# Order of the split weight products within a chunk: all products with the high parts first, those with the low parts last

## The chip, the cores and the metric

One core of a Trainium2 chip (trn2) runs the whole kernel; the other cores are idle. The metric is the device time of one execution in microseconds, lower is better. Engines are named as in the profile: PE is TensorE (PEld its weight loads), DVE VectorE, ACT ScalarE, POOL GpSimd, SP SyncE, which issues the weight loads from HBM.

## What is computed

One inference step of a two-layer decoder trunk on 256 prompt tokens and 8 single decode tokens, 264 columns in all, with a model width of 2048. Layer 0 is a gated DeltaNet mixer (32 value heads of 128) and a SwiGLU feed-forward layer; after it one shared K/V is projected; layer 1 is sliding-window attention (32 heads of 64, 4 K/V heads) and another feed-forward layer. Everything is float32.

```python
def trunk(x, prompt, ...):
    for i in range(N_A_LAYERS):
        h = rms_norm(x, norm_mix[i])
        y, conv_buf, S = deltanet_mixer(h, ..., w_in_a[i], ..., w_out_a[i])
        x = x + y
        x = x + swiglu_ffn(rms_norm(x, norm_ffn[i]), w_gate_up[i], w_down[i])
    kv = rms_norm(x, norm_kv) @ w_kv
    for j in range(N_B_LAYERS):
        q = (rms_norm(x, norm_mix[i]) @ w_q_b[j])
        o = swa_prompt(q, ...) if prompt else swa_sample(q, ...)
        x = x + o @ w_o_b[j]
        x = x + swiglu_ffn(rms_norm(x, norm_ffn[i]), w_gate_up[i], w_down[i])
    y = rms_norm(x, norm_final)
```

The nine weight matrices (`w_in`, `w_out`, `w_gate_up` and `w_down` of two layers, `w_kv`, `w_q`, `w_o`) make up most of the work, and they are all multiplied in the same way, by the function that is changed.

## The kernel before

**Chunks.** All weights are streamed in chunks of 128 x 1024 values, eight blocks of 128 x 128, 858 chunks in all. Each float32 value is split in two parts of a shorter format (fp32r), which TensorE multiplies in one pass: `split_hi` (L465, on ACT) writes `w_hi`, a rounded copy of `w_raw`, and raises `hi_ready`; `split_lo` (L472, on DVE) writes `w_lo` = `w_raw` - `w_hi` and raises `lo_ready`. The activations are split in the same way into `h_hi` and `h_lo` (in other stages `o_`, `a_`, `ao_`). A block of the product is then three products of 128 x 128 by 128 x 264, accumulated in one PSUM bank: w_hi by x_hi (L484), w_hi by x_lo (L485), w_lo by x_hi (L486). So a chunk is 24 products, each with its own weight load.

**Buffers.** `w_raw` has four buffers, `w_hi` and `w_lo` two each (`SPL`). Both splits of chunk c + 2 wait for `w_used` of chunk c, which the last product of a chunk raises (L490). SP's load of a chunk waits for `lo_ready` four chunks back (`load`, L497). Readers of finished banks also wait for `w_used`, or for later semaphores.

**`tiles`** (L475) issues the products of a chunk. `tl` lists its eight blocks: number of the block in the chunk, bank, the two activation parts, whether the block is the first or last one for its bank. Where other work of TensorE is woven in, a chunk is issued in two calls: with `part` 0, four blocks, and with `part` 1, the other four. With `part` None the whole chunk is issued at once (feed-forward layers, K/V, most of the out and o projections). `ends` is used for the very last chunk of the program alone, whose banks are read one by one.

**What stands between the halves.** In the DeltaNet stage (`turn`, L2094) PE works on the 12 chunks of a group of two heads, and weaves in the small products of the group before: `step(G, 2*j)` (L1911) ahead of the first half of chunk j and `step(G, 2*j + 1)` ahead of the second. The steps are one chain of small products with DVE and ACT in between: an inverse of a triangular matrix (steps 4 to 14), the recurrence over two blocks of tokens and the decode tokens (15 to 21), the outer products for the decode states and the sums of squares (21 to 23). Steps 0, 2, 3, 9 and 20 have no products. There are 16 groups. DVE and ACT have programs of their own with the same step numbers: in the turn of chunk j, ACT issues `split_hi` of chunk j + 1 and then its parts of steps 2j and 2j + 1 (in steps 4 and 16 the other way round), DVE its part of step 2j, then `split_lo` of chunk j + 1, the convolution of the next group's q, k and v (L2241), then step 2j + 1. On all engines the instructions run in the order in which they are written. The q projection and the first eight chunks of the o projection (L1112 to L1141) weave in the attention in the same way, with `attention(i, h)`; the first chunks of the program (`first_turn`, L2121) are cut in two because their activations come in two parts (`norm_lo`).

Names that the next sections use: L1709 is ACT's copy in step 12; L2310 DVE's transposes in the inverse; L1713 ACT's copy in step 14; L2379 DVE's `dec_sel` in step 18, and L2062 the products of step 19 that read it; L2405 the new state `S` of DVE in step 19, and L1909 the outer products of steps 21 to 23, the third of which, in step 21, waits for it; L1662 ACT's logarithm of the next group's sums of squares (step 22), for which L2081 waits in step 23; L1919 step 1, which waits for the normalised q and k (L2262); L993 and L773 the turning of the cached keys and the copy of it.

Of the kernel before, what the change touches and what calls it, by code (L numbers as in the profile page):

```python
# [13 lines left out]
P = 128  # L14
# [42 lines left out]
def yoco_step(nc, x_prompt, x_sample, state_delta, state_conv, cache_k, cache_v, norm_mix, norm_ffn,  # L57
# [6 lines left out]
    T = NP + NB  # L64
# [30 lines left out]
    SPL = 2  # L95
# [22 lines left out]
    with ctx:  # L118
# [8 lines left out]
        bank = lower + [upper[:, i, :] for i in range(4)]  # L127
# [18 lines left out]
        w_hi = sb("w_hi", [P, SPL, ELEMS], F32R)  # L146
        w_lo = sb("w_lo", [P, SPL, ELEMS], F32R)
# [95 lines left out]
        low = ExitStack()  # L243
        with low:
# [6 lines left out]
            part = sb("part", [P, 4, T], F32, low)  # L251
# [42 lines left out]
        hi_ready = sem("hi_ready")  # L294
        lo_ready = sem("lo_ready")
        w_used = sem("w_used")
# [177 lines left out]

        def tiles(pe, c, tl, part=None, ends=None):  # L475


            q, s = c
            if part in (None, 0):
                pe.wait_ge(lo_ready, 4 * q + (s + 1))  # L480
            for n, (t, bk, xh, xl, first, last) in enumerate(tl):
                wh = w_hi[:, s % SPL, t * P:(t + 1) * P]
                wl = w_lo[:, s % SPL, t * P:(t + 1) * P]
                nc.tensor.matmul(bank[bk][:, 0:T], wh, xh, start=first, stop=False)  # L484
                nc.tensor.matmul(bank[bk][:, 0:T], wh, xl, start=False, stop=False)  # L485
                m = nc.tensor.matmul(bank[bk][:, 0:T], wl, xh, start=False, stop=last)  # L486
                if ends is not None and last and n < len(tl) - 1:
                    m.then_inc(ends, 1)
            if part in (None, 1):
                m.then_inc(w_used, 1)  # L490
            return m

        def load(sp, c, *halves):

# [415 lines left out]
        def pe_after_delta(pe):  # L910
# [201 lines left out]
            for i in range(8):  # L1112
                for j in range(4):
                    c = chunk(C_Q, RAW, 0, 4 * i + j)
                    if j == 0:
                        pe.wait_ge(u_read, U_Q + i - 1)
                    if i == 0:
                        pe.wait_ge(unit_lo, split_count("mix1", j))
                    tl = [(2 * kk + n, (2 * (i % 2) if i else 6) + n, h_hi[:, 4 * j + kk, :], h_lo[:, 4 * j + kk, :],
                           j + kk == 0, 4 * j + kk == KT - 1) for kk in range(4) for n in range(2)]  # L1120
                    attention(i, 2 * j)
                    tiles(pe, c, tl[0:4], 0)
                    attention(i, 2 * j + 1)
                    tiles(pe, c, tl[4:8], 1)
            for j in range(8):
                c = chunk(C_O, RAW, 0, j)
                order = [(0, 0), (0, 1), (1, 0), (1, 1), (0, 2), (0, 3), (1, 2), (1, 3)] if j == 0 else [
# [5 lines left out]
                pe.wait_ge(p_lo, 2 * j + (2 if j == 0 else 1))  # L1133
                if j == 0:
                    pe.wait_ge(u_read, U_O - 1)
                tiles(pe, c, tl[0:4], 0)
                attention(8 + j // 4, 2 * (j % 4) + 1)
                if j == 0:
                    pe.wait_ge(u_read, U_O)
                pe.wait_ge(p_lo, 2 * j + 2)  # L1140
                tiles(pe, c, tl[4:8], 1)  # L1141
            columns(C_O, UNIT["o"], U_O, ao_hi, ao_lo, done=8)
            ffn(1)

# [672 lines left out]
        def _(pe):  # L1817
# [18 lines left out]
            for u in range(4):  # L1836
# [5 lines left out]
                             stop=True).then_inc(at_pe, 1)  # L1842
# [251 lines left out]
            def turn(g, G):  # L2094
                for j in range(12):
# [10 lines left out]
                    else:  # L2106
# [3 lines left out]
                        tl = [(2 * kk + n if u else 4 * n + kk, pair + n, h_hi[:, k + kk, :], h_lo[:, k + kk, :],  # L2110
                               k + kk == 0, k + kk == KT - 1) for kk in range(4) for n in range(2)]
                        c = chunk(C_IN, 12, g, j)
                    tiles(pe, c, tl[0:4], 0)
                    if G is not None:
                        step(G, 2 * j + 1)
                    if g is None and j == 0:
                        pe.wait_ge(unit_copied, 3 * GROUPS)
                    tiles(pe, c, tl[4:8], 1)

            def first_turn():  # L2120

                for j in range(12):
# [9 lines left out]
                           k + kk == 0, k + kk == KT - 1) for kk in range(4) for n in range(2)]  # L2132
                    if j < 4:
                        pe.wait_ge(norm_lo, 2 * j + 1)
                    tiles(pe, c, tl[0:4], 0)
                    if j < 4:
                        pe.wait_ge(norm_lo, 2 * j + 2)
                    tiles(pe, c, tl[4:8], 1)
                    if j in (1, 3):
                        b = j // 2  # L2140
                        tiles(pe, first_ba(b), [(t, 6, h_hi[:, 8 * b + t, :], h_lo[:, 8 * b + t, :], b + t == 0,
# [617 lines left out]
```

## Time and profile before

| | |
|---|---|
| time, median of 3 runs (lowest to highest) | 2893.99 us (2893.37 to 2894.33) |
| the profiled execution's own time | 2895.47 us |
| its span, first to last instruction | 2893.6 us |
| PE busy, products | 2870.3 us (99%), 25543 |
| DVE busy | 1795.9 us (62%) |
| ACT busy | 1418.8 us (49%) |
| mean busy share of the DMA engines on the weight queue | 56.9% |
| mean granted clock of TensorE, share of full speed | 0.998 |

How to read it: one execution is recorded, with the start and length of each instruction. A line such as L484 is a line of the program; since all weight products come from `tiles`, the three lines L484 to L486 hold 20,592 of them, and their operands' names tell the stage. The products are pipelined: each is drawn some 0.28 us long while the next one starts earlier, so a busy PE is not one that loses nothing, and the distance between starts has to be read. "upper" stands for PSUM banks of the upper half.

### The profile page before, as it was taken

The numbers are of one execution on the slowest core, as the hardware profiler recorded it, in microseconds if no ns is written. First come the engines' busy times: TensorE is split into PE (matmuls) and PEld (weight loads), VectorE is DVE, ScalarE is ACT, GpSimd is POOL, SyncE is SP. The second block draws the span as 40 slices with busy tenths as digits, with TensorE's granted clock in tenths as the row PEclk, the third lists the DMA queues.
The fourth block names the chain that finished last, engine by engine and source line by source line (L and its number), as shares of the span: only waits on it lengthen the run. The fifth ranks groups of instructions, "written<-read, shape, count | busy, mean of one in ns | idle before, by whom it ended". The sixth has DMA issues, their size and how long they took to land.

```text
span 2893.6 us, 68883 instructions
## 1 busy us (share of the span) xinstructions
PE 2870.3 (99%) x25543; PEld 2794.9 (97%) x25543; DVE 1795.9 (62%) x2868; ACT 1418.8 (49%) x2139; POOL 193.8 (7%) x301
## 2 busy tenths in 40 slices
PE   8999999999999999999999999999999999999999
PEld 7999999999999999999999999999999999999999
DVE  6778788788886455555555444577555555554444
ACT  6656566566564444444444344566444444444343
POOL 0212222122220000000000000000000000000000
PEclk9999999999999999999999999999999999999999
DMA  7666656656555556555555555744455555555554
GB/s 217 181 183 182 192 169 181 192 159 191 170 177 191 192 186 182 178 178 180 181 178 180 180 182 178 219 152 132 168 177 181 181 179 178 180 181 180 178 181 147
DMA packets 521090, 518.97 MB, mean 179 GB/s; under 512 B 32127, under 2 KB 444200, under 8 KB 520664
## 3 DMA queue, kind: packets, MB, share of 16 engines
q1 hardware_dynamic: 519150, 510.34, 56.9%
q0 software_dynamic: 1152, 5.58, 0.6%
q8 instruction: 147, 2.41, 0.4%
q14 instruction: 47, 0.39, 0.0%
q10 hardware_dynamic: 594, 0.25, 0.0%
HBM read 492.12 MB, written 32.82 MB: 181 GB/s over the span
## 4 chain that ended last, share of the span: by engine, by line
PE 67%; DVE 1%; ACT 1%; issue 0%; DMA 0%; DVEq 0%; ACTq 0%
PE bank L484 11%; PE bank L486 11%; PE bank L485 11%; PE upper L486 11%; PE upper L484 11%; PE upper L485 11%; PE upper L1013 0%; ACT w_hi L465 0%; PE upper L1037 0%; PE upper L1025 0%; DMA x_res<-x_spill 0%; DVE w_lo L472 0%; PE upper L1014 0%; PE upper L1150 0%; ACT scores L798 0%
## 5 line engine op out<-in xcount | busy, mean ns | idle before, releaser
L472 DVE TENSOR_TENSOR w_lo<-w_raw,w_hi 128x1024 fp32r<-128x1024 f32 x858 | 1049.7, 1223 | 933.5 <-ACT w_hi L465 929.0
L465 ACT ACTIVATE w_hi<-w_raw 128x1024 fp32r<-128x1024 f32 x858 | 908.8, 1059 | 1263.5 <-PE bank L486 736.0
L484 PE MATMUL bank<-h_hi,w_hi 128*128 128x264 f32 x3168 | 937.1, 296 | 3.4 <-DVE w_lo L472 3.4
L485 PE MATMUL bank<-h_lo,w_hi 128*128 128x264 f32 x3168 | 901.1, 284 | 0.0
L486 PE MATMUL bank<-h_hi,w_lo 128*128 128x264 f32 x3168 | 900.4, 284 | 0.0
L484 PEld LDWEIGHTS bank<-h_hi,w_hi 128*128 128x128 f32 x3168 | 598.0, 189 | 24.6 <-issue 12.1
L485 PEld LDWEIGHTS bank<-h_lo,w_hi 128*128 128x128 f32 x3168 | 598.8, 189 | 1.3
L486 PEld LDWEIGHTS bank<-h_hi,w_lo 128*128 128x128 f32 x3168 | 597.3, 189 | 0.0
L484 PE MATMUL upper<-h_hi,w_hi 128*128 128x264 f32 x1456 | 415.3, 285 | 0.0
L486 PE MATMUL upper<-h_hi,w_lo 128*128 128x264 f32 x1456 | 414.2, 284 | 0.0
L485 PE MATMUL upper<-h_lo,w_hi 128*128 128x264 f32 x1456 | 413.5, 284 | 0.0
L485 PEld LDWEIGHTS upper<-h_lo,w_hi 128*128 128x128 f32 x1456 | 275.2, 189 | 0.0
L486 PEld LDWEIGHTS upper<-h_hi,w_lo 128*128 128x128 f32 x1456 | 274.6, 189 | 0.0
L484 PEld LDWEIGHTS upper<-h_hi,w_hi 128*128 128x128 f32 x1456 | 274.5, 189 | 0.0
L485 PE MATMUL upper<-a_lo,w_hi 128*128 128x264 f32 x704 | 200.7, 285 | 0.0
L485 PE MATMUL bank<-a_lo,w_hi 128*128 128x264 f32 x704 | 200.7, 285 | 0.0
L486 PE MATMUL upper<-a_hi,w_lo 128*128 128x264 f32 x704 | 200.4, 285 | 0.0
L486 PE MATMUL bank<-a_hi,w_lo 128*128 128x264 f32 x704 | 200.4, 285 | 0.0
L484 PE MATMUL bank<-a_hi,w_hi 128*128 128x264 f32 x704 | 200.2, 284 | 0.0
L484 PE MATMUL upper<-a_hi,w_hi 128*128 128x264 f32 x704 | 200.1, 284 | 0.0
L484 PEld LDWEIGHTS bank<-a_hi,w_hi 128*128 128x128 f32 x704 | 132.5, 188 | 0.1
L485 PEld LDWEIGHTS upper<-a_lo,w_hi 128*128 128x128 f32 x704 | 132.6, 188 | 0.0
(429 smaller groups left out, 4057.3 us busy)
## 6 DMA issues: line engine op xcount, KB each, us to landing
w_raw<-in_w_gate_up_dram SPq DMA_DIRECT2D x704, 256.0 KB, 2.9
w_raw<-in_w_in_a_dram SPq DMA_DIRECT2D x388, 256.0 KB, 3.2
w_raw<-in_w_down_dram SPq DMA_DIRECT2D x352, 256.0 KB, 2.9
w_raw<-in_w_out_a_dram SPq DMA_DIRECT2D x128, 256.0 KB, 3.1
s_dec<-in_state_delta_dram SPq DMA_DIRECT2D x32, 512.0 KB, 5.7
out_dram<-s_dec SPq DMA_DIRECT2D x32, 512.0 KB, 5.0
w_raw<-in_w_q_b_dram SPq DMA_DIRECT2D x64, 256.0 KB, 3.2
w_raw<-in_w_o_b_dram SPq DMA_DIRECT2D x64, 256.0 KB, 2.9
```

The source lines that it names most:

```text
L465: nc.scalar.activation(w_hi[:, s % SPL, :], w_raw[:, s, :], ACT.Copy).then_inc(hi_ready, 1)
L472: ops.tensor_tensor(w_lo[:, s % SPL, :], w_raw[:, s, :], w_hi[:, s % SPL, :].bitcast(F32), ALU.subtract).then_inc(lo_ready, 1)
L484: nc.tensor.matmul(bank[bk][:, 0:T], wh, xh, start=first, stop=False)
L485: nc.tensor.matmul(bank[bk][:, 0:T], wh, xl, start=False, stop=False)
L486: m = nc.tensor.matmul(bank[bk][:, 0:T], wl, xh, start=False, stop=last)
```

## The change

In `tiles`, the products of a chunk are issued in another order. First come, block by block, the two products with `w_hi`; when all eight blocks have had them, the eight products with `w_lo` follow. The wait at the start is for `hi_ready` alone, and the wait for `lo_ready` stands ahead of the products with `w_lo`. A chunk in two calls has, with `part` 0, the eight products with `w_hi` of its first four blocks; with `part` 1, eight products with `w_hi` of the others and then all eight with `w_lo`: 8 and 16 products, where there were 12 and 12. The callers give the whole list `tl` to both calls; the other three places where they do so read as the one shown. With `ends` the old order stays. `w_used` is raised by the last product, as before.

```diff
@@ -474,21 +474,29 @@
         def tiles(pe, c, tl, part=None, ends=None):
-
             q, s = c
+            high = lambda t: w_hi[:, s % SPL, t * P:(t + 1) * P]
+            low = lambda t: w_lo[:, s % SPL, t * P:(t + 1) * P]
+            if ends is not None:
+                pe.wait_ge(lo_ready, 4 * q + (s + 1))
+                for n, (t, bk, xh, xl, first, last) in enumerate(tl):
+                    nc.tensor.matmul(bank[bk][:, 0:T], high(t), xh, start=first, stop=False)
+                    nc.tensor.matmul(bank[bk][:, 0:T], high(t), xl, start=False, stop=False)
+                    m = nc.tensor.matmul(bank[bk][:, 0:T], low(t), xh, start=False, stop=last)
+                    if last and n < len(tl) - 1:
+                        m.then_inc(ends, 1)
+                m.then_inc(w_used, 1)
+                return
             if part in (None, 0):
+                pe.wait_ge(hi_ready, 4 * q + (s + 1))
+            for t, bk, xh, xl, first, last in tl if part is None else tl[4 * part:4 * part + 4]:
+                nc.tensor.matmul(bank[bk][:, 0:T], high(t), xh, start=first, stop=False)
+                nc.tensor.matmul(bank[bk][:, 0:T], high(t), xl, start=False, stop=False)
+            if part in (None, 1):
                 pe.wait_ge(lo_ready, 4 * q + (s + 1))
-            for n, (t, bk, xh, xl, first, last) in enumerate(tl):
-                wh = w_hi[:, s % SPL, t * P:(t + 1) * P]
-                wl = w_lo[:, s % SPL, t * P:(t + 1) * P]
-                nc.tensor.matmul(bank[bk][:, 0:T], wh, xh, start=first, stop=False)
-                nc.tensor.matmul(bank[bk][:, 0:T], wh, xl, start=False, stop=False)
-                m = nc.tensor.matmul(bank[bk][:, 0:T], wl, xh, start=False, stop=last)
-                if ends is not None and last and n < len(tl) - 1:
-                    m.then_inc(ends, 1)
-            if part in (None, 1):
+                for t, bk, xh, xl, first, last in tl:
+                    m = nc.tensor.matmul(bank[bk][:, 0:T], low(t), xh, start=False, stop=last)
                 m.then_inc(w_used, 1)
-            return m
         def load(sp, c, *halves):
...
@@ -1119,9 +1127,9 @@
...
         def tiles(pe, c, tl, part=None, ends=None):
-                    tiles(pe, c, tl[0:4], 0)
+                    tiles(pe, c, tl, 0)
-                    tiles(pe, c, tl[4:8], 1)
```

What PE issues in the DeltaNet stage around steps 12 (L1984), 13 (L1994) and 14 (L2002), before; `waits` gives the semaphores that a product waits for, and lines of dots stand for products that go on in the same pattern:

```order
L1984 MATMUL upper<-Xm,Tm 32x32 [waits inv_dve]
...
L484 MATMUL bank0<-h_hi,w_hi 128x264 [waits lo_ready]
L485 MATMUL bank0<-h_lo,w_hi 128x264
L486 MATMUL bank0<-h_hi,w_lo 128x264
L484 MATMUL bank1<-h_hi,w_hi 128x264
L485 MATMUL bank1<-h_lo,w_hi 128x264
...
L486 MATMUL bank1<-h_hi,w_lo 128x264
L1994 MATMUL upper<-NT,Nm 64x64 [waits inv_dve,inv_act]
...
L484 MATMUL bank0<-h_hi,w_hi 128x264
L485 MATMUL bank0<-h_lo,w_hi 128x264
...
L486 MATMUL bank1<-h_hi,w_lo 128x264
L2002 MATMUL upper<-Xm,Tm 64x64 [waits inv_dve,inv_act]
```

And now (the same lines of the program are L1992, L2002 and L2010 there, and L493, L494 and L498 are the three products):

```order
L1992 MATMUL upper<-Xm,Tm 32x32 [waits inv_dve]
...
L493 MATMUL bank0<-h_hi,w_hi 128x264 [waits hi_ready]
L494 MATMUL bank0<-h_lo,w_hi 128x264
L493 MATMUL bank1<-h_hi,w_hi 128x264
...
L494 MATMUL bank1<-h_lo,w_hi 128x264
L2002 MATMUL upper<-NT,Nm 64x64 [waits inv_dve,inv_act]
...
L493 MATMUL bank0<-h_hi,w_hi 128x264
...
L494 MATMUL bank1<-h_lo,w_hi 128x264
L498 MATMUL bank0<-h_hi,w_lo 128x264 [waits lo_ready]
L498 MATMUL bank1<-h_hi,w_lo 128x264
...
L498 MATMUL bank1<-h_hi,w_lo 128x264
L2010 MATMUL upper<-Xm,Tm 64x64 [waits inv_dve,inv_act]
```

Between steps 12 and 13 stand eight products in place of twelve, and between 13 and 14 sixteen in place of twelve; the first product of the chunk waits for `hi_ready`, and `lo_ready` is waited for at the seventeenth.

The q projection, around the scores of one pair of heads (L1013), before:

```order
L484 MATMUL bank2<-h_hi,w_hi 128x264 [waits lo_ready,u_read]
L485 MATMUL bank2<-h_lo,w_hi 128x264
L486 MATMUL bank2<-h_hi,w_lo 128x264
...
L486 MATMUL bank3<-h_hi,w_lo 128x264
L1013 MATMUL upper<-kvT,qT 128x256 [waits u_read,t_copied]
...
L484 MATMUL bank2<-h_hi,w_hi 128x264
...
L486 MATMUL bank3<-h_hi,w_lo 128x264
L484 MATMUL bank2<-h_hi,w_hi 128x264 [waits lo_ready]
```

And now (the scores are L1021):

```order
L493 MATMUL bank2<-h_hi,w_hi 128x264 [waits hi_ready,u_read]
L494 MATMUL bank2<-h_lo,w_hi 128x264
L493 MATMUL bank3<-h_hi,w_hi 128x264
...
L494 MATMUL bank3<-h_lo,w_hi 128x264
L1021 MATMUL upper<-kvT,qT 128x256 [waits u_read,t_copied]
...
L493 MATMUL bank2<-h_hi,w_hi 128x264
...
L494 MATMUL bank3<-h_lo,w_hi 128x264
L498 MATMUL bank2<-h_hi,w_lo 128x264 [waits lo_ready]
```

The scores stand behind eight products of their chunk in place of twelve. The instruction streams of the other engines are the same in both kernels, and PE has the same number of register instructions, 22 and 10 of two kinds at the head of chunks in loops.

## Rows read from the trace of the kernel before

**Rows 1.** Page, part 1: busy us (share of the span) xinstructions

```profile
PE 2870.3 (99%) x25543; PEld 2794.9 (97%) x25543; DVE 1795.9 (62%) x2868; ACT 1418.8 (49%) x2139; POOL 193.8 (7%) x301
```

**Rows 2.** Windows: us, busy (xinstructions) of PE, PEld, DVE, ACT, POOL; PEclk, DMA, GB/s

```profile
1200.00:1500.00 300.00, 300.00 (x2467) 300.00 (x2466) 161.17 (x181) 122.22 (x129) 0.00 (x0) 1.00 0.59 180
```

**Rows 3.** Timeline, feed-forward: start us, us, engine, line, op, out<-in [idle<-releaser]

```profile
1301.08 1.06 ACT L465 ACTIVATE w_hi<-w_raw 128x1024 fp32r<-128x1024 f32 x1 [1.33 <-PE bank L486]
...
1302.26 1.23 DVE L472 TENSOR_TENSOR w_lo<-w_raw,w_hi 128x1024 fp32r<-128x1024 f32 x1 [1.01 <-ACT w_hi L465]
...
1303.67 0.28 PE L486 MATMUL bank<-h_hi,w_lo 128*128 128x264 f32 x1
...
1303.78 0.29 PE L484 MATMUL bank<-h_hi,w_hi 128*128 128x264 f32 x1
```

**Rows 4.** Waits of PE: who <- for what: us in total, times, longest

```profile
PE bank L484 <- DVE w_lo L472: 3.4, 3, 1.4
...
PE upper L1919 <- DVE qk L2262: 1.5, 1, 1.5
...
PE upper L484 <- DVE w_lo L472: 0.5, 1, 0.5
```

**Rows 5.** Timeline, first turn

```profile
31.51 1.04 ACT L465 ACTIVATE w_hi<-w_raw 128x1024 fp32r<-128x1024 f32 x1
...
33.95 0.36 PE L484 MATMUL bank<-h_hi,w_hi 128*128 128x264 f32 x1 [1.22 <-DVE w_lo L472]
...
36.01 1.04 ACT L465 ACTIVATE w_hi<-w_raw 128x1024 fp32r<-128x1024 f32 x1
...
38.46 0.36 PE L484 MATMUL bank<-h_hi,w_hi 128*128 128x264 f32 x1 [1.38 <-DVE w_lo L472]
```

**Rows 6.** Timeline, steps 11 and 13 of one group

```profile
356.55 0.45 DVE L2310 STREAM_TRANSPOSE Tm<-Um 128x256 f32<-128x256 f32 x1
...
357.60 0.44 PE L1976 MATMUL upper<-Um,Nm 32*32 32x32 f32 x16
...
360.87 0.31 ACT L1709 ACTIVATE Tm<-Tm 64x128 f32<-64x128 f32 x1
...
361.64 0.45 PE L1994 MATMUL upper<-NT,Nm 64*64 64x64 f32 x8
```

**Rows 7.** Timeline, step 15 of this group

```profile
364.74 0.54 ACT L1713 ACTIVATE NT<-upper 64x128 f32<-64x128 f32 x2
...
365.63 0.61 PE L2008 MATMUL upper<-vtok,NT 128*128 128x128 f32 x4
```

**Rows 8.** Timeline, step 19 of the group before

```profile
324.00 0.61 DVE L2379 SCALAR_TENSOR_TENSOR dec_sel<-masks,sc_eb,dec_qk 128x8 f32<-128x8 f32 x2
...
324.89 0.51 PE L2062 MATMUL upper<-dec_sel,Pb 128*128 128x8 f32 x4
```

**Rows 9.** Timeline, step 21 of that group

```profile
327.67 0.61 DVE L2405 SCALAR_TENSOR_TENSOR S<-S,egR,upper 128x128 f32<-128x128 f32 x2
...
328.24 0.64 PE L1909 MATMUL upper<-dec_dr,kmask 96*128 96x256 f32 x4
```

**Rows 10.** Timeline, step 23 of that group

```profile
332.04 0.83 ACT L1662 ACTIVATE qk_sq<-upper,bias_c 128x264 f32<-128x264 f32 x2
...
333.02 1.13 PE L2081 MATMUL upper<-norm_sq,masks 128*128 128x264 f32 x4
```

**Rows 11.** Timeline, attention stage, turning of the cached keys

```profile
1869.80 0.58 ACT L773 ACTIVATE k_t<-bank 128x508 f32<-128x508 f32 x1
...
1870.47 0.60 PE L993 MATMUL upper<-masks,k_win 127*128 127x127 f32 x4
```

**Rows 12.** Single lines: xcount: ns min/median/max, first and last start us

```profile
L480 PEldq EVENT_SEMAPHORE  x105: 51/51/51, 19.6 to 2815.0; - x105
...
L946 PEldq COMPARE_BRANCH  x20: 76/208/239, 1155.6 to 2619.6; - x20
...
L2062 PE MATMUL upper<-dec_sel,Pb x64: 172/256/256, 115.8 to 901.0; 128*128 128x8 f32 x64
```

More of the change, by code:

```diff
@@ L1121, in pe_after_delta @@
                     attention(i, 2 * j)
-                    tiles(pe, c, tl[0:4], 0)
+                    tiles(pe, c, tl, 0)
                     attention(i, 2 * j + 1)
-                    tiles(pe, c, tl[4:8], 1)
+                    tiles(pe, c, tl, 1)
             for j in range(8):
@@ L1135, in pe_after_delta @@
                     pe.wait_ge(u_read, U_O - 1)
-                tiles(pe, c, tl[0:4], 0)
+                tiles(pe, c, tl, 0)
                 attention(8 + j // 4, 2 * (j % 4) + 1)
@@ L1140, in pe_after_delta @@
                 pe.wait_ge(p_lo, 2 * j + 2)
-                tiles(pe, c, tl[4:8], 1)
+                tiles(pe, c, tl, 1)
             columns(C_O, UNIT["o"], U_O, ao_hi, ao_lo, done=8)
@@ L2112, in turn @@
                         c = chunk(C_IN, 12, g, j)
-                    tiles(pe, c, tl[0:4], 0)
+                    tiles(pe, c, tl, 0)
                     if G is not None:
@@ L2117, in turn @@
                         pe.wait_ge(unit_copied, 3 * GROUPS)
-                    tiles(pe, c, tl[4:8], 1)
+                    tiles(pe, c, tl, 1)
             def first_turn():
@@ L2134, in first_turn @@
                         pe.wait_ge(norm_lo, 2 * j + 1)
-                    tiles(pe, c, tl[0:4], 0)
+                    tiles(pe, c, tl, 0)
                     if j < 4:
                         pe.wait_ge(norm_lo, 2 * j + 2)
-                    tiles(pe, c, tl[4:8], 1)
+                    tiles(pe, c, tl, 1)
                     if j in (1, 3):
```

## The prediction

> **What bounds the kernel now.** I read the page's busy shares first: TensorE is busy for 99% of the span at the full 2.4 GHz (granted clock 1.00 in the stretch of [rows 2]), VectorE for 62%, ScalarE for 49% [rows 1]. The stretches come next: between 1200 and 1500 us TensorE starts 2467 products in 300 us [rows 2], one per 121.6 ns, and the last product of a chunk and the first of the next, with other weights and another bank, keep the same distance: 1303.67 to 1303.78 [rows 3]. With 858 chunks of 24 products this is 20,592 x 0.1216 = 2504 us of 2893.6. So time can only be won or lost in two ways: the spacing, or waits of TensorE. The waits view lists few of them: 3.4 us in three places for w_lo, 0.5 us once more [rows 4]. Since each product is drawn 0.28 us long at a spacing of 0.12, a wait under some 0.16 us shows as no idle time at all; therefore I go to the timeline for how early each operand is ready.
>
> Where nothing stands between chunks (feed-forward layers), w_hi is made at 1301.08 to 1302.14, w_lo at 1302.26 to 1303.49, and the chunk that uses both starts at 1303.78 [rows 3]: a lead of 0.29 us. w_lo is nowhere late there, so the later need of it wins nothing.
>
> **The change part by part.**
>
> *Count.* Each chunk still has 16 products with w_hi and 8 with w_lo, 24 weight loads, and as many register instructions. The second wait rides on a product that exists already. ACT, DVE, POOL and SP keep their streams; both w_hi and w_lo of a chunk are still released by w_used at its end, so splits and loads are set off where they were. Count term: 0.
>
> *The wait for w_lo moves back by 16 products, 1.95 us.* This frees the three waits of [rows 4]. At 33.95 TensorE had waited 1.22 us; w_hi was there at 32.55. At 38.46 it had waited 1.38 us; w_hi was there only at 36.01 + 1.04 = 37.05 [rows 5]. The first gain is swallowed by the second, which can start at about 37.10: 1.36 us together. The third is 3.4 - 1.22 - 1.38 = 0.8 us, with w_hi long there, and the one of 0.5 us goes too: -2.6 us. (All four added up, with nothing swallowed, would be -3.9 us.)
>
> *The halves become uneven.* In the DeltaNet stage (and in the q and o projections) small products, the steps, stand ahead of each half of a chunk. Between an even step and the odd one behind it there were 12 products; now there are 8. Between an odd step and the next even one there are 16. So each odd step is reached 4 x 0.122 = 0.49 us earlier after its even step, and 0.49 us more lies behind it. TensorE takes products in order, so an odd step whose operand is not there holds everything behind it. The operands of an odd step are mostly made by ACT or DVE from the even step before; these do not move. For each odd step I take the lead (end of the instruction that releases it, to the start of the product that waits) and look whether its engine waited for an odd step, since then it would come earlier as well:
> - step 13: ACT's copy ends at 361.18, the product starts at 361.64 [rows 6]: lead 0.46.
> - step 15: ACT ends at 365.28, product 365.63 [rows 7]: lead 0.35.
> - step 19: dec_sel ends at 324.61, its product starts at 324.89 [rows 8]: lead 0.28.
> - step 21: S ends at 328.28; the group starts at 328.24 and its third product, which needs S, about 328.47 [rows 9]: lead 0.19.
> - step 23: ACT's second logarithm ends at 332.87, the product starts at 333.02 [rows 10]: lead 0.15.
>
> None of the five releasing rows has brackets, that is, its engine was at work right up to it (on a split, or on DVE's other work): the queue sets its time, and it does not move.
>
> The other odd steps have longer leads, the shortest of them step 11 (357.00 to 357.60, 0.60 [rows 6]); they cost 0. A product cannot start the moment its operand is written. How long it takes at least the trace shows only from above: 0.09 us from the end of k_t (1870.38) to the transpose at 1870.47, with no idle time in front of it [rows 11]. I take 0.08. The new stall is 0.49 - lead + 0.08: 0.11, 0.22, 0.29, 0.38, 0.42, together 1.42 us per group of heads. There are 16 groups (the 64 products of dec_sel [rows 12] are 4 a group): **+22.7 us**. With 0 in place of 0.08 it is 1.02 x 16 = 16.3. Above, the first product after a real wait helps: at 33.95 it is drawn 0.36 us long instead of 0.28 [rows 5], so up to 0.05 more may be lost behind a wait; with 0.13 it is 1.67 x 16 = 26.7.
>
> The Trainium skill ("TensorE: Matmul & The Clock Gate", section "Architectural detail: the array is 16× 32×32, not 1× 128×128") says that the queue may pull weight loads ahead of products in flight, while products stay in order. By it the load of the waiting product might lie outside the lag, and the sum would be the one with 0; the 0.09 of the row, from which I take 0.08, neither proves nor excludes that.
>
> Could the stalls be given back? Even steps now get 0.49 us more, but only their stalls could shrink, and the waits view has almost none there [rows 4]. DVE and ACT make up nothing: TensorE is the bound and every stall moves w_used with it.
>
> *Single places.* The first group's step 1 already waits 1.5 us for qk [rows 4] and now 0.49 more; among the small products of the attention stage two pairs (k_t as above, with a lead of 0.09 [rows 11], and the last head's values) cost about 0.48 each, four in all: +2.4 us.
>
> Sum: -2.6 + 22.7 + 2.4 = **+22.5 us**. The profiled execution took 2895.47 us around a span of 2893.6; it lies 1.5 us above the median of the runs, 2893.99. On the median: **2916.5 us**, 0.8% slower.
>
> **The rivals.**
>
> *B, the operands come along (not slower).* If what releases an odd step is itself set off by the odd step before, it also comes earlier and the leads survive. Then only -2.6 us remains, and some single places: 2891.4 to 2894. It decides from the point where the shift is no more than the lead, that is 0.49 against 0.15 to 0.46. Against it: in all five places the releasing engine was at work just before, not waiting for an odd step. For it: I followed one group of sixteen closely. 9%.
>
> *C, the spacing shrinks (faster).* Products with the same weights now stand in pairs and the low ones eight in a row. A spacing shorter by 1 ns would give 20.6 us, so it takes 1.4 ns to beat the old kernel by 0.2% in spite of the stalls; with 2 ns the time is 2916.5 - 41 = 2875. Against it: the change of weights and bank costs nothing that shows: 0.11 us [rows 3] against the mean of 0.1216, and changes of weights are as many as before. 3%.
>
> *D, the new wait costs by itself (much slower).* If each mid-chunk wait held the sequencer for the 51 ns that a separate one takes [rows 12], 858 x 0.051 = 44 us would be added: 2960. Against it: the wait is part of a weight load, and where the loop's branch takes 208 ns [rows 12] the spacing of products does not open. 4%.
>
> The forecast, A, has 84%.
>
> **How the numbers follow.** A gives 2916.5. Its bounds are 2893.99 - 3.9 + 16.3 + 2.4 = 2908.8 and 2893.99 - 2.6 + 26.7 + 2.4 = 2920.5; the spacing may move by 0.3 ns either way from what else runs at the time (20,592 x 0.3 ns = 6 us): 2903 to 2927, with B, C and D outside, 16% together. A measurement of this kernel can tell about 0.2% (5.8 us) from no change. Slower by more than that: A and D, 0.88. Within: B, 0.09. Faster: C, 0.03.
>
> **What would show it.** In the changed profile the three waits for w_lo before 60 us are gone; spacing in the feed-forward layers stays 121.6 ns; the distance between the same step in two groups, (901.0 - 115.8) / 15 = 52.35 us now [rows 12], grows by about 1.4; DVE and ACT busy times stay. In front of steps 15, 19, 21 and 23 (dec_sel, S, the logarithm) the distances between products open by 0.2 to 0.5 us, and TensorE's waits view begins to list them. It would be wrong if a group keeps its length, if the feed-forward stretches change theirs, or if even steps get stalls.

## The result and the profile after

The changed kernel takes 2922.4 us, the median of four runs (2921.75 to 2924.68); the kernel before takes 2894.16 in four runs beside it (2893.37 to 2895.25). The ratio is 1.0098, with an interval of 1.0083 to 1.0112: 28.2 us slower. The forecast was 2916.5 in a range of 2903 to 2927. The profiled run took 2921.75 us around a span of 2919.9, 26.3 more than the span before. The profiled run of before (2895.47) lay 1.3 us above the 2894.16, and that of the changed kernel 0.65 us below its median, which is why the medians differ by a little more. In the diffs and rows that follow, line numbers of the changed kernel are 8 higher than before in the steps: L2387 makes `dec_sel` (L2379), L2070 reads it (L2062), L2063 is the product with `intraT` (L2055), L1431 makes `intraT` (L1423). The weight products are L493 and L494 (high part) and L498 (low part); four chunks at the end of the program, not only the last one, go through `ends` and keep the old order.

The page of the changed kernel, busy times:

```profile
PE 2875.7 (98%) x25543; PEld 2789.0 (96%) x25543; DVE 1799.6 (62%) x2868; ACT 1418.0 (49%) x2139; POOL 169.1 (6%) x301
```

The work is the same as in [rows 1], instruction for instruction; TensorE is busy for 98% instead of 99% of a longer span. DVE and ACT do as much as before. Only POOL's busy time has moved, from 193.8 to 169.1 us, which the forecast had not asked about; half of it turns out to belong to the largest single loss.

The stretch in the feed-forward layers (columns as in [rows 2]):

```profile
1200.00:1500.00 300.00, 300.00 (x2471) 300.00 (x2470) 160.11 (x181) 123.08 (x129) 0.00 (x0) 1.00 0.59 180
```

The granted clock is 1.00 there as before, and TensorE starts 2471 products where it started 2467.

TensorE's waits after the change:

```profile
PE upper L2070 <- DVE dec_sel L2387: 16.4, 14, 1.2
PE upper L1827 <- DMA x_rows_d<-in_x_sample_dram: 5.7, 1, 5.7
PE upper L1902 <- issue: 2.7, 16, 0.2
PE upper L1033 <- DVE ao_lo L2639: 2.3, 5, 0.5
PE upper L1927 <- DVE qk L2270: 2.1, 1, 2.1
...
PE bank L493 <- ACT w_hi L465: 1.1, 1, 1.1
```

The waits for `w_lo` of [rows 4] are gone, and one for `w_hi`, 1.1 us at 37.15 us, stands in their place:

```profile
37.15 0.36 PE L493 MATMUL bank<-h_hi,w_hi 128*128 128x264 f32 x1 [1.13 <-ACT w_hi L465]
```

Step 1 of the first group waits 2.1 us instead of 1.5. New at the top is step 19 waiting for `dec_sel`, fourteen times by up to 1.2 us, and step 5 (L1902), sixteen times by up to 0.2.

Where the time went I read from the end of each chunk, after less before, in the two profiled runs:

| stretch (time before) | shift gained, us | the forecast's term |
|---|---|---|
| start to the end of the first turn, 71 us | -2.25 | waits for `w_lo`: -2.6 |
| first step 1, chunk 14 | +0.5 | +0.49 |
| the turns with steps, 78 to 911 us | +34.4 | +22.7 |
| spacing from 911 us to the end | -6.0 | 0 |
| attention (q and o projections) | +1.0 | +1.9 |
| last chunk to the end of the span | -1.3 | 0 |
| sum | +26.3 | +22.5 |

The tail is TensorE's clock and not the order. In the profile of before the granted clock is 0.50 (1.2 GHz) for a while shortly before the end, where TensorE had been busy without a gap since 2860 us; in the changed kernel's it stays at 1.00 there. Columns as in [rows 2]:

```profile
2882.70:2886.10 3.40, 3.40 (x18) 3.40 (x18) 1.07 (x3) 1.84 (x6) 0.00 (x0) 0.50 0.00 0
```

18 products start there, where 28 fit at the full clock: 1.2 us.

Inside the turns the distance between the same step of two groups tells the price:

```profile
L2070 PE MATMUL upper<-dec_sel,Pb x64: 173/256/277, 114.1 to 933.2; 128*128 128x8 f32 x64
```

(933.2 - 114.1) / 15 = 54.61 us, against 52.35 in [rows 12]: +2.26 a group, where 1.4 was forecast. The same by the ends of chunks, mean over fourteen groups, puts a place to each part: the chunk with **step 5** +0.25, **step 15** +0.28, **step 19** +1.46, **step 23** +0.31; every other chunk is within 0.03 of what it was, those of steps 13 and 21 included. The two groups left out differ at step 19: 0.12 in the first, and 0.01 in the last, behind which no next group is prepared.

**Step 19** first. One group of the changed kernel, timeline from 330 us:

```profile
330.78 0.39 PE L2063 MATMUL upper<-intraT,vn 128*128 128x128 f32 x2
...
331.02 1.70 DVE L2387 SCALAR_TENSOR_TENSOR dec_sel<-masks,sc_eb,dec_qk 128x8 f32<-128x8 f32 x2
...
331.43 1.27 POOL L1431 TENSOR_TENSOR intraT<-ET,masks 128x512 f32<-128x512 f32 x1
...
332.77 0.61 PE L2070 MATMUL upper<-dec_sel,Pb 128*128 128x8 f32 x4 [1.17 <-DVE dec_sel L2387]
```

and the same place in the kernel before ([rows 8] has the `dec_sel` there: 324.00, 0.61 us for the pair):

```profile
324.76 2.14 POOL L1423 TENSOR_TENSOR intraT<-ET,masks 128x512 f32<-128x512 f32 x1 [0.31 <-PE upper L2055]
...
325.67 1.52 DVE L2241 SCALAR_TENSOR_TENSOR cacc<-craw,convw,cacc 128x264 f32<-128x264 f32 x1
```

POOL builds the next group's `intraT` in the buffer that PE's L2063 reads in step 19. Before, that read was POOL's releaser, and came after `dec_sel` was done. Now step 19 begins 0.49 us earlier, PE has read the buffer when POOL comes free, and POOL starts at 331.43, 0.02 us behind the start of the second `dec_sel`. (The row draws the pair as one; the second starts at 331.41.) That `dec_sel` ends at 332.72 and POOL at 332.70: an operation on 128x8 numbers has taken as long as POOL's on 128x512. Its durations in the whole run (min/median/max in ns), after and then before:

```profile
L2387 DVE SCALAR_TENSOR_TENSOR dec_sel<-masks,sc_eb,dec_qk x32: 213/473/1304, 113.5 to 932.5; 128x8 f32<-128x8 f32 x32
```

```profile
L2379 DVE SCALAR_TENSOR_TENSOR dec_sel<-masks,sc_eb,dec_qk x32: 212/224/475, 114.7 to 899.8; 128x8 f32<-128x8 f32 x32
```

And POOL's, after and then before:

```profile
L1431 POOL TENSOR_TENSOR intraT<-ET,masks x16: 1262/1265/2360, 72.9 to 877.8; 128x512 f32<-128x512 f32 x16
```

```profile
L1423 POOL TENSOR_TENSOR intraT<-ET,masks x16: 1275/2140/2140, 75.2 to 847.8; 128x512 f32<-128x512 f32 x16
```

Before, it was POOL that was stretched, and after it DVE's L2241, which nobody waits for. The collision is not new; the change has moved it onto the one operation that TensorE waits for next. The 16 masks take 33.1 us before and 21.3 after, which is 11.8 of the 24.7 us that POOL is busy for less; most of the rest, 10.7 us, is a 128x32 copy (at 345.15 in that group: 1.03 us, beside `w_lo`; 0.27 in the changed kernel). DVE's busy time hides the change: `dec_sel` gained 15.2 us and L2241, 15 times at 1.52 us before and at 0.49 now, lost 14.5.

**Step 5**, the odd step that the forecast passed over. Before, from 344 us:

```profile
344.39 0.37 DVE L2311 TENSOR_TENSOR Xm<-Pb,masks 128x256 f32<-128x256 f32 x1
...
345.03 0.46 PE L1894 MATMUL upper<-Pb,PbT 64*64 64x64 f32 x16
```

and after:

```profile
353.17 0.38 DVE L2319 TENSOR_TENSOR Xm<-Pb,masks 128x256 f32<-128x256 f32 x1
...
353.66 0.46 PE L1902 MATMUL upper<-Pb,PbT 64*64 64x64 f32 x16 [0.17 <-issue]
```

The lead was 345.03 - 344.76 = 0.27 us, shorter than that of step 19; now 0.11 us is left, and the rule of the forecast gives 0.49 - 0.27 + 0.08 = 0.30 for it. It costs less because here the operand came along a little: counted from the first weight product of its chunk, the mask product of DVE ends 1.30 us behind it, where it was 1.39. **Step 15** is as foretold: ACT's copy ends at 374.42 and the product starts at 374.47, behind a distance of 0.31 us from the product ahead instead of 0.12:

```profile
373.88 0.54 ACT L1721 ACTIVATE NT<-upper 64x128 f32<-64x128 f32 x2
...
374.16 0.28 PE L494 MATMUL bank<-h_lo,w_hi 128*128 128x264 f32 x1
...
374.47 0.60 PE L2016 MATMUL upper<-vtok,NT 128*128 128x128 f32 x3
```

The weight load of the waiting product starts at 374.47 too: it does not run ahead of the wait.

**Step 13** loses nothing, and the reason is that the forecast took the wrong operand for it. The program lets step 13 wait for ACT's copy of step 11 and DVE's product of step 12; L1709, ACT's copy of step 12, is for step 14. Before, DVE's operation is

```profile
360.20 0.58 DVE L2350 TENSOR_SCALAR NT<-upper 32x128 f32<-32x128 f32 x2 [0.71 <-PE upper L1984]
```

and ends at 360.78, 0.86 us ahead of the product at 361.64, not 0.46. After:

```profile
369.35 0.58 DVE L2358 TENSOR_SCALAR NT<-upper 32x128 f32<-32x128 f32 x2 [0.75 <-PE upper L1992]
...
370.02 0.31 ACT L1717 ACTIVATE Tm<-Tm 64x128 f32<-64x128 f32 x1
...
370.30 0.45 PE L2002 MATMUL upper<-NT,Nm 64*64 64x64 f32 x8
```

The product starts 0.03 us before the copy (now L1717) ends, so it did not wait for it.

### The profile page after: what moved, and what is told of

It reads as the page before. It is cut to its first block, busy times and chain, and to the rows that moved or that the text cites. A ratio compares the mean times of both kernels' runs of the same rounds, so it can differ in the third digit from the quotient of the medians.

```text
span 2919.9 us, 68883 instructions
## 1 busy us (share of the span) xinstructions
PE 2875.7 (98%) x25543; PEld 2789.0 (96%) x25543; DVE 1799.6 (62%) x2868; ACT 1418.0 (49%) x2139; POOL 169.1 (6%) x301
## 4 chain that ended last, share of the span: by engine, by line
PE 90%; ACT 4%; DVE 3%; issue 2%; DVEq 0%; ACTq 0%; DMA 0%
PE bank L493 18%; PE bank L498 17%; PE bank L494 16%; PE upper L498 10%; PE upper L493 10%; PE upper L494 10%; PE upper L1902 2%; ACT w_hi L465 1%; DVE dec_sel L2387 1%; PE upper L2089 1%; ACT L1656 1%; DVE cacc L2249 0%; PE upper L1927 0%; PE upper L2016 0%; PE upper L1021 0%
## 5 line engine op out<-in xcount | busy, mean ns | idle before, releaser
L493 PE MATMUL bank<-h_hi,w_hi 128*128 128x264 f32 x3168 | 829.2, 295 | 1.3 <-ACT w_hi L465 1.1
L494 PE MATMUL bank<-h_lo,w_hi 128*128 128x264 f32 x3168 | 794.1, 284 | 0.0
L493 PEld LDWEIGHTS bank<-h_hi,w_hi 128*128 128x128 f32 x3168 | 597.0, 188 | 22.0 <-issue 8.8
L494 PEld LDWEIGHTS bank<-h_lo,w_hi 128*128 128x128 f32 x3168 | 597.5, 189 | 1.4
L498 PE MATMUL bank<-h_hi,w_lo 128*128 128x264 f32 x3168 | 450.2, 284 | 0.0
L498 PEld LDWEIGHTS bank<-h_hi,w_lo 128*128 128x128 f32 x3168 | 412.5, 188 | 0.0
L493 PE MATMUL upper<-h_hi,w_hi 128*128 128x264 f32 x1456 | 361.7, 285 | 0.0
L494 PE MATMUL upper<-h_lo,w_hi 128*128 128x264 f32 x1456 | 361.4, 284 | 0.0
L493 PEld LDWEIGHTS upper<-h_hi,w_hi 128*128 128x128 f32 x1456 | 274.3, 188 | 0.0
L494 PEld LDWEIGHTS upper<-h_lo,w_hi 128*128 128x128 f32 x1456 | 273.9, 188 | 0.0
L498 PE MATMUL upper<-h_hi,w_lo 128*128 128x264 f32 x1456 | 206.6, 284 | 0.0
L498 PEld LDWEIGHTS upper<-h_hi,w_lo 128*128 128x128 f32 x1456 | 189.3, 188 | 0.0
L493 PE MATMUL bank<-a_hi,w_hi 128*128 128x264 f32 x688 | 170.9, 284 | 0.0
L493 PE MATMUL upper<-a_hi,w_hi 128*128 128x264 f32 x688 | 170.9, 284 | 0.0
L494 PE MATMUL bank<-a_lo,w_hi 128*128 128x264 f32 x688 | 170.7, 284 | 0.0
L494 PE MATMUL upper<-a_lo,w_hi 128*128 128x264 f32 x688 | 170.7, 284 | 0.0
L493 PEld LDWEIGHTS bank<-a_hi,w_hi 128*128 128x128 f32 x688 | 129.7, 189 | 0.0
L493 PEld LDWEIGHTS upper<-a_hi,w_hi 128*128 128x128 f32 x688 | 129.7, 189 | 0.0
L494 PEld LDWEIGHTS upper<-a_lo,w_hi 128*128 128x128 f32 x688 | 129.5, 188 | 0.0
L494 PEld LDWEIGHTS bank<-a_lo,w_hi 128*128 128x128 f32 x688 | 129.5, 188 | 0.0
```

The lines of the kernel that those rows point to most:

```text
L493: nc.tensor.matmul(bank[bk][:, 0:T], high(t), xh, start=first, stop=False)
L494: nc.tensor.matmul(bank[bk][:, 0:T], high(t), xl, start=False, stop=False)
L498: m = nc.tensor.matmul(bank[bk][:, 0:T], low(t), xh, start=False, stop=last)
```

## The experiments

Nine kernels, each timed against the kernel before on the same chip; since the kernel before gave 2895.2 to 2895.4 us there, and 2894.16 beside the changed kernel, kernels are best compared by their ratios. All compute the whole reference.

| kernel | median, us | before | ratio |
|---|---|---|---|
| POOL's mask behind `dec_sel` | 2908.69 | 2895.33 | 1.0049 [1.0035, 1.0063] |
| turns in halves, old order | 2887.61 | 2895.33 | 0.9975 [0.9965, 0.9985] |
| turns in halves, new order in each | 2888.42 | 2895.33 | 0.9976 [0.9967, 0.9985] |
| before, halves of 3 and 5 blocks | 2923.16 | 2895.33 | 1.0096 [1.0081, 1.0112] |
| only the chunk of step 19 in halves | 2905.71 | 2895.17 | 1.0040 [1.0027, 1.0054] |
| 16 products ahead of the odd step | 2888.69 | 2895.17 | 0.9975 [0.9966, 0.9984] |
| q and o projections in halves too | 2887.48 | 2895.17 | 0.9975 [0.9965, 0.9984] |
| one wait, at the chunk's start | 2893.03 | 2895.17 | 0.9990 [0.9981, 0.9999] |
| three passes over the blocks | 2890.04 | 2895.36 | 0.9982 [0.9973, 0.9992] |

### Is it POOL that makes step 19 late?

The changed kernel with one more wait on POOL, for the step 18 of DVE in which `dec_sel` is made:

```
                 after(pool, seq_pe, 7 * (g - 1) + 6)
+                after(pool, dec_dve, 11 * (g - 1) + 10)
                 pool.tensor_tensor(intraT[:, :, :], ET[:, :, :], bc(incl, 1, 4), ALU.mult).then_inc(incl_ready, 1)
```

> The changed kernel with one more wait on POOL: its mask of the next group's intraT (L1431) starts only when DVE's second dec_sel (step 18) is done; nothing else moves. Theory P (POOL and DVE collide): step 19 is late because that POOL instruction now starts 0.02 us after DVE's second dec_sel and the latter then takes 1.30 us in place of 0.21; with the wait it takes 0.21 again, the stall of step 19 falls from 1.46 us to about 0.3 a group (0.49 - 0.28 + 0.08), 16 groups: about -18 us, 2903 to 2907. Rival Q (queue alone: DVE is late with dec_sel whatever POOL does, only because step 19 is reached earlier): dec_sel stays at 1.3 us and the time at 2922.

Measured 2908.69 us, ratio 1.0049: 13.4 us over its kernel before, where the change had 28.2, and 1.7 above the expected 2903 to 2907. The waits for `dec_sel` have left the list of TensorE's waits. The two lines in question:

```profile
L2388 DVE SCALAR_TENSOR_TENSOR dec_sel<-masks,sc_eb,dec_qk x32: 213/224/473, 116.2 to 920.0; 128x8 f32<-128x8 f32 x32
```

```profile
L1432 POOL TENSOR_TENSOR intraT<-ET,masks x16: 1267/2206/2212, 74.0 to 866.7; 128x512 f32<-128x512 f32 x16
```

`dec_sel` is back at its old durations and POOL takes 2.2 us again. Step 19's chunk now costs +0.37 instead of +1.46, near the forecast 0.29, and the others stay (step 5 0.25, step 15 0.28, step 23 0.25, step 21 0.05). So 1.09 of step 19's 1.46 us is the collision, and its mechanism is shown by its removal. The gain is 14 x 1.09 = 15.3 us by this sum (the first and the last group have no such loss), and 28.2 - 13.4 = 14.8 by the medians. The profiled run itself shows less, because at the end of chunk 14 it is 2.65 us later than the changed kernel's, at places that the edit does not touch. 1.6 of that is the granted clock, which fell behind the wait of 2.1 us at step 1 in this run and not in the changed kernel's, whose wait was as long:

```profile
74.80:78.20 3.40, 3.40 (x16) 3.07 (x15) 3.35 (x5) 1.99 (x5) 2.41 (x5) 0.50 0.88 231
```

At the same place of the changed kernel's run (73.8 to 77.2 us) the clock is 1.00 and 30 products start instead of 16. The other 1.0 us came before 71 us, where the profiled runs differ by as much among themselves (below).

### Distance or order?

Two kernels put the DeltaNet turns back to 12 products ahead of an odd step and 12 behind it, the first in the old order (high, high, low, block by block), the second with the eight high products of each half ahead of its four low ones, and a `w_lo` wait behind the first eight. The call and the second helper:

```
-                    tiles(pe, c, tl, 0)
+                    by_half(pe, c, tl[0:4], 0)
...
-                    tiles(pe, c, tl, 1)
+                    by_half(pe, c, tl[4:8], 1)
```

```
            if part == 0:
                pe.wait_ge(hi_ready, 4 * q + (s + 1))
            for t, bk, xh, xl, first, last in tl:
                nc.tensor.matmul(bank[bk][:, 0:T], high(t), xh, start=first, stop=False)
                nc.tensor.matmul(bank[bk][:, 0:T], high(t), xl, start=False, stop=False)
            if part == 0:
                pe.wait_ge(lo_ready, 4 * q + (s + 1))
            for t, bk, xh, xl, first, last in tl:
                m = nc.tensor.matmul(bank[bk][:, 0:T], low(t), xh, start=False, stop=last)
```

> The changed kernel, but in the DeltaNet turns alone the old order (12 products on each side of an odd step, three products per block). Theory D (distance): all of the loss sits in these turns, the gains outside stay: -2.3 us up to 71 us and some -5 us of shorter spacing behind the stage, +1 in attention: 2894 - 6 = 2886 to 2890. Rival (the new order costs elsewhere too, for example through the second wait): 2894 or more.

> The changed kernel, but in the DeltaNet turns each half holds 12 products again, in the new order within a half (eight high, then four low). Theory D (only the distance from an even to an odd step matters): as the run with the old order in the turns, 2886 to 2890. Rival O (the order itself, high first and low last, costs in the turns): near 2922, or between the two.

Measured 2887.61 and 2888.42, which their intervals don't tell apart. In both the chunks of a group keep the length they had before within 0.04 us. The stalls come from the distances 8 and 16, and not from the order in which high and low follow each other. The other way round, the kernel before, in its old order and with its single wait, with its halves made uneven:

```
-                    tiles(pe, c, tl[0:4], 0)
+                    tiles(pe, c, tl[0:4 if g is None else 3], 0)
...
-                    tiles(pe, c, tl[4:8], 1)
+                    tiles(pe, c, tl[4 if g is None else 3:8], 1)
```

> The kernel before, old order of the products, but in the DeltaNet turns the halves are 3 and 5 blocks (9 and 15 products) in place of 4 and 4: an odd step is reached 3 x 0.122 = 0.365 us earlier. Theory D with P: step 5 +0.12, step 15 +0.16, step 23 +0.19, step 19 +1.4 a group (POOL is free 0.05 us after the second dec_sel starts, so they collide here too): 1.9 x 16 = 30 us, 2920 to 2926; without the collision at step 19 only +9 us, 2903. Rival O (order, not distance): 2894.

Measured 2923.16, ratio 1.0096: as slow as the change, without any of its new order. Its waits:

```profile
PE upper L2062 <- DVE dec_sel L2379: 14.8, 14, 1.1
...
PE bank L484 <- DVE w_lo L472: 3.3, 3, 1.3
```

It has the waits for `w_lo` at the start too, which the change has not. By chunks: step 5 +0.11, step 15 +0.18, step 19 +1.34, step 23 +0.22. The odd steps are 3 x 0.122 = 0.37 us early here and 0.49 in the change, 0.12 less, and each stall is 0.09 to 0.14 smaller: the stall grows about one for one with the distance, as the rule of the leads has it. About 1.5 us of the total are not the distance: the clock fell to 0.50 behind step 1 here as well, from 76.9 to 80.3 us. Behind the turns its shift stays at +27.2 to +27.4 us, so this kernel shows no shorter spacing.

### Where is step 21's stall?

Only the chunk that carries steps 18 and 19 is cut in halves of 12, all others keep 8 and 16:

```
-                    tiles(pe, c, tl, 0)
+                    (by_half(pe, c, tl[0:4], 0) if j == 9 else tiles(pe, c, tl, 0))
```

> The changed kernel, but the one chunk of each turn around step 19 (the tenth) is cut into 12 and 12 products again (eight high, four low); all other chunks stay at 8 and 16. Theory D with P: only the 1.46 us of step 19 go, 16 x 1.46 = 23 us: 2898 to 2901, and the other steps keep their 0.24, 0.28 and 0.31 us. Rival (the delays of a group are tied to each other, so that DVE, relieved at step 19, makes another step late, step 21 first of all, for which 0.38 us had been forecast and nothing was seen): 2903 to 2906.

Measured 2905.71. Step 19 costs 0.02 now, and **step 21 costs 0.41** where the changed kernel has none; step 23 falls to 0.05. The higher of the two expectations holds. The group that shows it, weight loads of L1934 (steps 21 to 23; the columns are busy time and mean ns, then the idle time before them and its releasers):

```profile
L1934 PEld LDWEIGHTS upper<-dec_dr,kmask 96*128 96x128 f32 x128 | 20.5, 189 | 6.1 <-DVE S L2430 4.5 <-DVE s_dec L2440 0.4
```

In the changed kernel the same group (L1917) has 1.3 us before it and `S` is not named. So the forecast 0.38 for step 21 was right for a kernel whose step 19 is in time; in the real one the 1.46 lost two steps earlier had already given `S` its time. Less is enough: in the run with POOL's wait, 0.37 lost at step 19 leaves 0.05 at step 21.

### Do even steps mind?

The turns with all 16 high products ahead of the odd step and the 8 low ones behind it, so that the even steps are reached 0.49 us earlier instead:

```
            for t, bk, xh, xl, first, last in tl if part == 0 else ():
                nc.tensor.matmul(bank[bk][:, 0:T], high(t), xh, start=first, stop=False)
                nc.tensor.matmul(bank[bk][:, 0:T], high(t), xl, start=False, stop=False)
            if part == 1:
                pe.wait_ge(lo_ready, 4 * q + (s + 1))
            for t, bk, xh, xl, first, last in tl if part == 1 else ():
                m = nc.tensor.matmul(bank[bk][:, 0:T], low(t), xh, start=False, stop=last)
```

> The changed kernel, but in the DeltaNet turns the halves are the other way round: all 16 products with w_hi ahead of the odd step, the 8 with w_lo behind it. An even step is now reached 0.49 us earlier after its odd step. Theory D (what counts is the engine between: an even step is late only where DVE or ACT waited for the odd step before it): step 15 to 16 alone (DVE had waited 0.18 us for step 15, and its last result is 0.09 us ahead of step 16): 0.48 us x 16 = 8 us over the run with halves of 12, 2896 to 2899. Rival N (any step with a short lead loses what it is short of; steps 16, 18 and 22 have leads of 0.04 to 0.11 us): 0.48 + 0.46 + 0.49 = 1.43 us x 16 = 23 us, 2911.

Measured 2888.69: nothing is lost, and no chunk of a group grows by more than 0.03. (The last group keeps 8 and 16 in this kernel.) That excludes the rival's 2911 as well as my 2896 to 2899. I had expected a stall at step 16, from a lead that I took from the wrong product: the third product of step 16 does not wait for `dec_qk`. With its true operand, `vn`, the lead that is left in this kernel is 366.39 - 365.98 = 0.41 us. Which product of a step waits for what has to be read for each, in the waits of the program and in the trace. At step 18, one of the rival's, `vn` ends 0.12 us ahead of the product (371.70, 371.82), as it did before (321.08, 321.19), although the step now follows step 17 by 0.49 us less. The even steps stand at the chunk boundaries, and `w_used`, raised there, sets off the splits of DVE and ACT too; so moving the odd step between two boundaries leaves the even step and its operand where they were.

### What the rest of the change is worth

The q and o projections in halves as well, so that only chunks without steps keep the new order whole:

```
                     attention(i, 2 * j)
-                    tiles(pe, c, tl, 0)
+                    by_half(pe, c, tl[0:4], 0)
                     attention(i, 2 * j + 1)
-                    tiles(pe, c, tl, 1)
+                    by_half(pe, c, tl[4:8], 1)
```

> The run with halves of 12 in the DeltaNet turns, and halves of 12 in the q and o projections too (eight high, four low each). Theory D: the 1.0 us that the attention stage lost by the distance goes as well: 2887 to 2888, the fastest so far. Rival (that 1.0 us is the order's): no change against the run with halves of 12 in the turns alone, 2888.4.

Measured 2887.48. The +1.0 us of the attention stage is gone (by the ends of chunks), but in the whole time this kernel, the two with halved turns and the one with 16 and 8 can't be told apart.

Then, on top of halved turns, the wait for `w_lo` back at the chunk's start everywhere, where the old kernel has it:

```
             if part in (None, 0):
-                pe.wait_ge(hi_ready, 4 * q + (s + 1))
+                pe.wait_ge(lo_ready, 4 * q + (s + 1))
...
-                pe.wait_ge(lo_ready, 4 * q + (s + 1))
```

> The run with halves of 12 in the DeltaNet turns, new order everywhere, but each chunk waits for lo_ready at its start, as before the change, and for nothing in its middle. Theory S (the shorter spacing behind the DeltaNet stage, some -5 us, comes from the order of the products, and the later wait gives only the -2.1 us before 71 us and 0.6 at 922): 2891. Rival W (the spacing comes from the wait): back to 2894 to 2895.

Measured 2893.03, between the two expectations. The waits are back as before the change:

```profile
PE bank L493 <- DVE w_lo L472: 2.9, 3, 1.4
```

At 71 us this kernel is 0.54 us later than the kernel before, that with the later wait 2.09 earlier: 2.6 us between these two profiled runs, as forecast. One pair says it no closer than about 1 us: of all eleven profiled runs, the eight with the later wait are 1.1 to 2.5 us earlier than that of before at this point (mean 1.8), the other two 0.15 and 0.54 later. Between the means of the two kinds lie 2.1 us. Of the shorter spacing most stays: between the chunks ending at 946 and 1864 us of the kernel before it gains 2.0 us, the one with the later wait 2.7. Last, the order inside the chunks without steps changed once more, all 8 products with `xh`, then 8 with `xl`, then the low ones:

```
-            for t, bk, xh, xl, first, last in tl if part is None else tl[4 * part:4 * part + 4]:
+            some = tl if part is None else tl[4 * part:4 * part + 4]
+            for t, bk, xh, xl, first, last in some:
                 nc.tensor.matmul(bank[bk][:, 0:T], high(t), xh, start=first, stop=False)
+            for t, bk, xh, xl, first, last in some:
                 nc.tensor.matmul(bank[bk][:, 0:T], high(t), xl, start=False, stop=False)
```

> The run with halves of 12 in the DeltaNet turns; elsewhere the chunk goes in three passes over its blocks (w_hi by x_hi for all, w_hi by x_lo for all, w_lo by x_hi for all), so that no two neighbouring products share their weights or their bank. What is asked: whether the 0.2 to 0.3 ns by which the products behind the DeltaNet stage stand closer in the new order than in the old has to do with neighbours that share weights or bank. If sharing shortens the distance: these stretches lose the 4 us again or more, 2892 or above. If it lengthens it: 2 us or more are won, 2886 or less. If it is neither: 2888 within 1.5 us, and the cause stays open.

Measured 2890.04, between the expectations for "neither" and for a loss. The same stretch gains 2.1 us instead of 2.7, so pairs with one weight tile account for 0.6 of it at most. What makes the products 0.3 to 0.4 ns closer stays open: the order of high and low is part of it, since the old order with other halves gains nothing there, and the later wait is the smaller part.

## Why the prediction was right in direction, and where its terms were off

- **What bounds.** Right. TensorE's order with its distances sets the time; the sum of stalls and of spacing accounts for all but the 1.3 us of the tail, which is the clock.
- **The waits for `w_lo`, -2.6.** Right: -2.25 in the changed kernel, with the second wait limited by `w_hi` as foretold; about 2.1 over all profiled runs.
- **Odd steps early by 0.49.** The mechanism is right, and the uneven halves alone make it. So is the rule "0.49 - lead + 0.08" where a step is undisturbed: step 15 0.28 for 0.22; step 21, in the kernel that relieves step 19, 0.41 for 0.38; step 19, with POOL out of the way, 0.37 for 0.29. Step 23 gave 0.31 for 0.42, because ACT's second logarithm did move: it ends 1.38 us behind the first weight product of its chunk, where it was 1.56.
- **Step 13, 0.11.** The operand was the wrong one: the copy that ends at 361.18 is for step 14. The right one had a lead of 0.86 us, and the step costs nothing: 1.8 us too much in the sum.
- **"The other odd steps have longer leads, the shortest of them step 11 ... they cost 0."** This failed. Step 5 had 0.27 us, with the mask product of DVE as its latest operand, and costs 0.25. It adds about 4 us.
- **Step 19, 0.29.** This is the mis-sized term: 1.46, because `dec_sel` itself became slower. The forecast said that what releases the odd steps "does not move", since each releasing engine was busy up to it. It did not ask what the earlier step 19 lets start: POOL's mask, which then held DVE. Fourteen groups at 1.46 us and one at 0.12 against sixteen at 0.29 are 16 us too little, of which the run with POOL's wait shows 15 to be the collision.
- **Step 21, 0.38.** It did not appear, because a stall of 1.46 just ahead had absorbed it: about 6 us too much. Stalls of neighbouring steps don't add up when the earlier one also gives time to the later one's operand.
- **Single places, +2.4.** +0.5 at step 1 was right, attention cost 1.0 for 1.9.
- **"The spacing stays."** Off by 0.4 ns a product behind the turns, -6.0 us in all, just the bound that the range had for it.

The term of the turns was 11.7 us too small and the spacing 6.0 too high, so that a total near the truth (28.2 for 22.5 us) owes something to errors of both signs. Rival B had a small part of the truth: the operands of step 5 and of step 23 came 0.09 and 0.18 us earlier. Rival C had the right sign, with 6.0 us where it needed 1.4 ns a product or 28.8 us. Rival D is excluded: chunks without steps have the mid-chunk wait and became shorter.

## What to carry to other kernels

Where a hand-made order puts small dependent work between pieces of a long stream, the length of each piece is a deadline: reordering the inside of a piece is nearly free; changing its length is free only where the step behind it has lead to spare (16 and 8 products cost nothing here, 8 and 16 cost 34 us). Before moving work, list for every step the lead of each operand that the program makes it wait for, the shortest included, and then ask what the moved step releases on the other engines and what that will collide with. Here the later need for `w_lo` was worth having; with the halves kept at 12 and 12 it makes the kernel 0.25% faster (2887.5 us) instead of 1% slower.

## What the runs showed of the hardware

- **DVE and POOL hold each other up, whole instructions long.** A DVE operation on 128x8 numbers took 1.30 us instead of 0.21 because POOL's on 128x512 started 0.02 us behind it; with POOL second, behind `w_lo` of 1.21 us, POOL's took 2.14 to 2.21 instead of 1.27. The Trainium skill ("SBUF — State Buffer", section "Who interferes with whom") says that a DVE instruction with two inputs in SBUF contends with a GpSimd instruction that reads SBUF, and that the order of issue, not the shape, decides who is blocked. The rows agree on the first. On the order they agree where `w_lo`, drawn at 324.54, holds POOL's mask, drawn at 324.76; where `dec_sel` is drawn at 331.41 and POOL at 331.43, the one drawn first is the one held. The first `dec_sel` of the pair is still drawn until 331.49, so the second may have come to the port behind POOL; no run here shows when an instruction takes it.
- **The lag from an operand to its product.** Where a step waits, the product is drawn 0.05 us behind the end of its operand at steps 15, 19 and 21, 0.11 at step 5 and 0.15 at step 23. Measured stall less 0.49 plus lead, which also holds what is lost just behind the wait, gives 0.14 at step 15 and 0.11 at step 21; at step 5 it gives 0.03 because the operand moved.
- **The granted clock can halve in one run and not in the next.** Behind a wait of 2.1 us at step 1 it fell to 0.50 from 74.8 to 78.2 us in the run with POOL's wait, at a cost of 1.6 us, and stayed at 1.00 behind the same wait in the changed kernel's. Stretches of this kind make differences of 1 to 2 us between single profiled runs that no edit explains.
- **The spacing of products depends a little on their order**: 6.0 us in the 15,600 products behind the turns, attention's own loss apart, 0.4 ns each of 121.6; in the stretch from 946 to 1864 us 2.7 us, the same in all seven profiled runs with the new order and the later wait there, 0.04 in the old order with other halves. The cause is open.
